# One gelu step of ScalarE placed behind the copies of the S5 output table, and the split weights requested two chunks further in SyncE's queue, in a two-layer hybrid decoder

## What is computed

```python
h = rms_norm(x, norm_g) * (1.0 + scale) + shift
proj = h @ w_in
(hg_q, hg_f, hg_i, hg_g, at_q, at_k, at_v, at_g,
 ix_q, ix_k, ix_w, s5_u, s5_g, merge_g) = split_cols(proj)
ya = hgrn2_mixer(hg_q, hg_f, hg_i, lb, hg_onorm_g) * jax.nn.silu(hg_g)
yb = dsa_mixer(at_q, at_k, at_v, ix_q, ix_k, ix_w, positions, at_qnorm_g, at_knorm_g) * jax.nn.silu(at_g)
yc = s5_mixer(s5_u, s5_a_re, s5_a_im, s5_log_dt, s5_b_re, s5_b_im, s5_c_re, s5_c_im, s5_d, s5_glu_w, s5_glu_b) * jax.nn.silu(s5_g)
yd = jnp.einsum('bsnw,nwd->bsnd', ys, w_branch)
merged = jnp.einsum('bsnd,bsnd->bsd', gates, yd)
return x + gate * (merged @ w_out)
```

## Time and profile before

| what | value |
|---|---|
| median of 3 runs | 1184.42 us (1183.04 to 1185.35) |
| the profiled execution, its own time | 1182.32 us |
| its span, first to last instruction | 1180.5 us |
| PE busy | 1145.6 us (97% of the span) |
| DVE busy | 887.4 us (75%) |
| ACT busy | 519.9 us (44%) |
| POOL busy | 495.6 us (42%) |
| mean TensorE clock granted | 0.995 of full |
| chain that ended last, by engine | PE 73%, DVE 14%, issue 4%, ACT 4%, DMA 3%, POOL 1% |

### The profile page before, as it was taken

One profiled execution on the slowest core, in us unless ns is written; L12 is line 12 of the kernel. 1 busy time (PEld: TensorE's weight loads), 2 busy tenths in 40 slices (PEclk: granted clock), 3 DMA queues, 4 the chain that ended last, 5 costly groups with the idle time before them and its releaser, 6 DMA issues.

```text
span 1180.5 us, 19604 instructions
## 1 busy us (share of the span) xinstructions
PE 1145.6 (97%) x7796; PEld 912.2 (77%) x7796; DVE 887.4 (75%) x1435; ACT 519.9 (44%) x864; POOL 495.6 (42%) x336
## 2 busy tenths in 40 slices
PE   6999999999999989999999999999999999899998
PEld 3797787887788778788768777878777878788887
DVE  4697898857489988788947589988746899778242
ACT  5554326754444344443244642456453445444321
POOL 0143451343363554545416344323425536445451
PEclk9999999999999999999999999999999999899999
DMA  9632221141322535763615222212323434366322
GB/s 353 243 129 72 74 73 55 54 142 55 107 66 71 136 105 168 260 253 109 248 36 179 90 66 77 76 54 71 116 65 99 108 91 118 109 214 218 104 72 72
DMA packets 63451, 141.88 MB, mean 120 GB/s; under 512 B 29440, under 2 KB 31744, under 8 KB 62592
## 3 DMA queue, kind: packets, MB, share of 16 engines
q1 hardware_dynamic: 54016, 137.48, 35.3%
q10 hardware_dynamic: 9344, 3.15, 1.1%
HBM read 127.76 MB, written 10.49 MB: 117 GB/s over the span
## 4 chain that ended last, share of the span: by engine, by line
PE 73%; DVE 14%; issue 4%; ACT 4%; DMA 3%; POOL 1%; SPq 1%; DVEq 0%; ACTq 0%
PE bank L1677 21%; PE bank L1679 20%; PE bank L1678 20%; PE bank L1820 2%; PE bank L1830 1%; PE bank L1844 1%; DMA raw<-in_wfull 1%; DMA arena<-in_wada 1%; DVE arena L1177 1%; PE bank L1872 1%; DVE arena L1176 1%; DVE arena L1237 1%; ACT w_hi L765 1%; DVE arena L1469 1%; DVE arena L1213 1%
## 5 line engine op out<-in xcount | busy, mean ns | idle before, releaser
L731 POOL TENSOR_TENSOR w_lo<-raw,w_hi 128x512 fp32r<-128x512 f32 (+1 forms) x166 | 248.0, 1494 | 664.3 <-ACT w_hi L765 664.3
L1677 PE MATMUL bank<-h_hi,w_hi 128*128 128x512 f32 x896 | 358.9, 401 | 1.4 <-POOL w_lo L732 1.4
L1679 PE MATMUL bank<-h_hi,w_lo 128*128 128x512 f32 x896 | 349.2, 390 | 0.0
L1678 PE MATMUL bank<-h_lo,w_hi 128*128 128x512 f32 x896 | 349.1, 390 | 0.0
L765 ACT ACTIVATE w_hi<-raw 128x1024 fp32r<-128x1024 f32 (+2 forms) x170 | 178.5, 1053 | 241.7 <-PE bank L1679 154.0
L732 POOL TENSOR_TENSOR w_lo<-raw,w_hi 128x512 fp32r<-128x512 f32 (+2 forms) x166 | 255.2, 1537 | 0.0
L1677 PEld LDWEIGHTS bank<-h_hi,w_hi 128*128 128x128 f32 x896 | 168.2, 188 | 42.4 <-issue 6.3
L1678 PEld LDWEIGHTS bank<-h_lo,w_hi 128*128 128x128 f32 x896 | 168.3, 188 | 35.9 <-issue 2.4
L1679 PEld LDWEIGHTS bank<-h_hi,w_lo 128*128 128x128 f32 x896 | 168.2, 188 | 35.8
L1677 PE MATMUL bank<-w_hi,h_hi 128*128 128x512 f32 (+1 forms) x256 | 97.1, 379 | 1.9 <-DVE h_lo L1324 0.9
L1678 PE MATMUL bank<-w_lo,h_hi 128*128 128x512 f32 (+1 forms) x256 | 94.8, 370 | 0.0
(11 more groups left out here) (283 smaller groups left out, 1665.1 us busy)
## 6 DMA issues: line engine op xcount, KB each, us to landing
raw<-in_wfull SPq DMA_DIRECT2D x170, 512.0 KB, 4.0
arena<-in_wada SPq DMA_DIRECT2D x48, 512.0 KB, 5.2
x_scratch<-xm SPq DMA_DIRECT2D x2, 2048.0 KB, 9.2
arena<-x_scratch SPq DMA_DIRECT2D x2, 2048.0 KB, 9.7
arena<-in_x SPq DMA_DIRECT2D x4, 512.0 KB, 6.5
arena<-in_s5m SPq DMA_DIRECT2D x2, 1024.0 KB, 6.3
u_scratch<-arena ACTq DMA_DIRECT2D x4, 512.0 KB, 4.6
arena<-u_scratch SPq DMA_DIRECT2D x8, 256.0 KB, 3.0
```

The source lines that it names most:

```text
L731: nc.gpsimd.tensor_tensor(lo[:, :half], raw_chunk(n)[:, :half], hi[:, :half].bitcast(F32), ALU.subtract)
L1677: mm(out_, a_hi, b_hi, start=first, stop=False)
L1678: mm(out_, a_hi, b_lo, start=False, stop=False)
L1679: return mm(out_, a_lo, b_hi, start=False, stop=last)
```

## The change

Two edits. The step `gelu(0, 1)` moves from ahead of `cm("mg1", 3, 0)` to behind `s5(3, 1)` and `tab(3, 3)`. SP's bound on requested weights grows by two chunks at every step.

```diff
-        steps += gelu(0, 0) + tab(3, 1) + cm("wb1", 2) + s5(2, 4) + load("ysave", 2) + tab(3, 2) + gelu(0, 1) + cm("mg1", 3, 0)
-        steps += s5(3, 1) + tab(3, 3) + load("yback", 2) + load("mtin", 3, 0) + gelu(1, 0) + cm("mg1", 3, 1) + s5(3, 2) + load("mtin", 3, 1)
+        steps += gelu(0, 0) + tab(3, 1) + cm("wb1", 2) + s5(2, 4) + load("ysave", 2) + tab(3, 2) + cm("mg1", 3, 0)
+        steps += s5(3, 1) + tab(3, 3) + gelu(0, 1) + load("yback", 2) + load("mtin", 3, 0) + gelu(1, 0) + cm("mg1", 3, 1) + s5(3, 2) + load("mtin", 3, 1)
...
             for step in STEPS:
-                sent = weights(min(len(CHUNKS), FIRST[step] + len(chunks_of(step)) + RAW_SLOTS - 1), sent)
+                sent = weights(min(len(CHUNKS), FIRST[step] + len(chunks_of(step)) + RAW_SLOTS + 1), sent)
```

## The result

The changed kernel takes 1167.32 us (median of 4 runs, 1167.25 to 1168.60), the kernel before on the same chip 1184.69 (4 runs, 1183.04 to 1185.35): a ratio of 0.986, 95% interval 0.985 to 0.987. It gains 17.4 us; 10.8 were forecast, and the time lies 2.2 us under the lower end of the range. The direction was right, the size wrong by a wide margin.

What follows compares the result with a forecast made beforehand. PE was taken as the bound, with DVE as much so up to line 1178. Terms 6.7 + 2.6 + 1.4 + 0.6 - 0.5 = 10.8 us took the median from 1184.42 to 1173.6 us, range 1169.5 to 1179.5.

Steps and rivals of the forecast that it cites:

- A: PE's 3.35 us stall per layer at `s5(3, 2)` (line 1943) goes once the sigmoid is behind the copies: 6.7 us gained.
- B: TensorE's clock no longer drops to half behind layer 1's stall at line 1943: 2.6 us gained.
- C: Chunk 64 is requested earlier, so PE's wait for its low half goes, in layer 0 only: 1.4 us gained.
- D: PE's waits for late chunk 52 and its layer 1 twin go, DVE's chain shortens little: 0.6 us gained, bounds 0 and 2.7.
- E: POOL's split of chunk 59 now runs beside DVE's angles and slows DVE: 0.5 us lost over both layers, bounds 0 and -3.
- F: Transfers held behind two more chunk requests (first `uin` of a layer, conditioning weights) still come in time: cost 0.
- R1: Rival: in the S5 stage DVE replaces the stall as splits move onto its busy stretches: 1179.6 us, chance 0.13.
- R2: Rival: each layer's held first `uin` load comes too late, PE waits 8.1 us per layer: 1189.8 us, chance 0.05.
- R3: Rival: the K and `wt` copies stay late for another reason, both stalls at `s5(3, 2)` stay: 1183.0 us, chance 0.05.

## Why the prediction was wrong

**A, the stall: right** for this profile. The copies of line 985 were forecast near 433 and stand at 430.46, with no wait behind them. DVE can turn the result at 436.14 where 438.3 was forecast. But the 6.7 us are those of one execution: the two stalls were 4.7 us in the second profile of the kernel before (3.33 + 1.35).

**B, the clock: right for the pair of profiles, too small in general.** The drop is gone, and nothing fell elsewhere. That the sum met the pair was luck in part: the three profiles have one drop, two and one. Drops also followed waits that B did not look at (for chunk 64, at line 1927), so it was a cost of all stalls, not of the two at line 1943.

**C: right** in layer 0, though not by the requests alone: with the move alone that wait is gone too. "Layer 1 has no such wait" was true of one execution only: it is 1.16 us there in both later profiles.

**D: the step that failed.** I wrote that DVE's chain "is shortened only by what the late chunk did to it: part of the 1.03 us gap at the scan", and took 0.6. Measured, D is 3.0 in the profiled pair, above its own upper bound of 2.7, which had left out layer 1's 0.24; against the second profile of the kernel before it is 5.1 (0.99 + 0.18 + 0.95 + 3.01). The gap was the wrong place to look: it is still 0.88 us in the changed kernel. What shrank is the way between the scans, by 4.3 us in layer 0 (19.5 to 15.2) and 3.7 in layer 1. Late data held ACT, ACT's copies of the K table held SP (its transfers of line 686 went out at 399.66, and at 396.59 after the change), and SP's next request for a chunk was late as well (402.21, and 399.14 at the same place of its queue after the change). Meanwhile DVE was slowed by the pile of splits, so that it looked busy. With POOL's share cut away and the data still late, 4.75 us of DVE's time showed up as a wait. The sign that I named for D, a longer wait at line 1927, did not come: that wait is gone. The earlier trace rows held the sign of the slowing, 1.78 us for line 1205 beside a split and 0.69 without: I used it in E to price a split that moves onto DVE, and did not ask which splits move away. Because I priced D low, I also missed that the queue's edit alone would halve the stall that A gives to the move.

**E: mechanism right, cost to PE nil.** Lines 1205 to 1208 took 0.68, 1.41 and 1.66 us at 428.94 beside chunk 59's split, 1.9 us more than before where 1.5 was forecast. Line 1205 itself, named as the sign, kept its 0.68 us. DVE still had 0.95 us to wait for PE's product, so nothing of it reached PE.

**F: right.** The first `uin` went out at 342.71 (342 was forecast) and nobody waited. The held load of conditioning weights cost DVE 0.88 us at 515.75, and the wait of 4.32 us at line 1596, now at 525.71, was unchanged.

**The step from the profile to the median: the second failure.** I subtracted the same 10.8 us from both and took the 2.1 us between them as a constant. The two later profiles say that they were not: PE's waits are 1.6 and 2.3 us longer there than in the first one (at line 1927 and at chunk 64 of layer 1), with one or two drops of the clock, and the change removes all of it. That fits the 2.3 us by which the medians gained more (17.4 - 15.1); two executions are few to call it the whole of them.

**The rivals.** R1 was aimed at the right resource with the wrong sign: in what was the stretch of 12.5 us, fewer splits lie beside DVE after the change, not more. By the section of the Trainium skill named there (GPSIMD Engine Reference, Specifications) POOL and DVE contend for SBUF; the runs agree, 12.5 us of DVE with POOL busy beside it against 6.7 with its splits cut. R2 did not occur: PE has no wait in the S5 stages. R3 fell: the move alone gives 7.9 us.

## What to carry to other kernels

When a late input is made early, look at what its lateness had pushed together: work on a second engine that arrives in a heap can slow a third one, and that cost stands in no table of waits. An engine without gaps is not thereby at its shortest; compare like instructions in it, and ask what ran beside the long ones. Where two causes hold the same step within half a microsecond, removing one shows nothing: test each with the other gone before you name the larger. And profile a kernel with stalls more than once: a term read from one execution is a sample, and the median's distance from it may be part of what the change removes.

## What the runs showed of the hardware

- **A DVE instruction that starts under a split of POOL is longer by what is left of the split, not by a ratio.** The forecast scaled by 2.6. The rows above show line 1240's 0.69 us becoming 1.66, line 1207's 0.43 becoming 1.39 and the scan's 1.21 becoming 2.30: each about 1 us more, whatever its length. But it is less where the split is nearly over:

```profile
409.40 1.30 POOL L732 TENSOR_TENSOR w_lo<-raw,w_hi 128x512 fp32r<-128x512 f32 x1
...
410.21 1.04 DVE L1228 TENSOR_TENSOR arena<-arena 128x512 f32<-128x512 f32 x1
```

  Here 0.49 us of POOL's instruction were left (to 410.70), and DVE's took 0.35 more than its 0.69. The same holds for the DVE instructions of the S5 stages (330 to 460 and 905 to 1040 us) that read SBUF and no bank and start under a split, more than 0.15 us before its end: in 60 of 61 in the kernel before, and in all 59 in the changed one, the excess over the shortest like instruction is what is left of POOL's instruction less 0.07 to 0.23 us. Those that already ran when a split began kept their length, 45 of 46 in the two kernels; the scan at 392.80 is one, with POOL starting at 392.86. So each instruction of POOL delays at most about one of DVE: six of POOL between 392 and 405, and six of DVE too long.
- **Instructions that read a bank of PSUM did not stretch.** None of the 38 that start under a split in the same windows of the two kernels did. In the changed kernel line 1213 took the usual 0.69 us at 404.69 although POOL was at work:

```profile
404.31 1.50 POOL L731 TENSOR_TENSOR w_lo<-raw,w_hi 128x512 fp32r<-128x512 f32 x1 [6.09 <-ACT w_hi L765]
404.69 0.69 DVE L1213 TENSOR_TENSOR arena<-bank,arena 64x512 f32<-64x512 f32 x1
```

- **The clock fell to half during or just behind idle times of 1.76 us and more, in some executions and not in others.** Three profiles of one kernel have the drops in three different sets of places; of two equal waits of 3.35 us in one execution one brought a drop (layer 1) and one did not (layer 0), and in the third profile the one in layer 0 did. The low clock then lasted 3 to 7 us. In the S5 stages of all profiles here, waits of 1.72 us and less were followed by none. At the start of the kernel, too, the low clock lasted longer in some executions: most of a difference of 2.1 us that no edit made (349.45 against 347.32 above).
